# Splitting the dense matmuls of up and down into two 64-row matmuls, in a two-layer decoder kernel on one core

## The chip, the cores and the metric

The kernel runs on one core of a Trainium2 chip. The metric is device time in microseconds of one execution; lower is better.

## What is computed

Two layers act on 288 token columns (256 of a prompt, 32 of eight samples), d_model 1024. A layer adds to x the output of four token mixers (linear attention, spatial gating, a convolution module, sliding-window attention), gated and projected, and then a SwiGLU block. The change touches the second half alone:

```
x = x + merged @ w_out
g, up = split(rmsnorm(x, norm2_g) @ w_gate_up, 2)      # 1024 -> 2 x 2816
x = x + (silu(g) * up) @ w_down                        # 2816 -> 1024
```

## The kernel before, in words

Everything is kept transposed: features on the 128 partitions, the T = 288 tokens along the free axis. So a dense product is a row of tiles of 128 output features, and each tile accumulates over the input features in chunks of 128 (`u`): 8 chunks for `up` (KC), 22 for `down` (HC).

All arithmetic is float32 to the last bits that matter. An operand is split in two float32r parts, hi and lo, and each product of a chunk is three matmuls (lines 410 to 416, `split_mm`): w_hi by x_hi, w_hi by x_lo, w_lo by x_hi, all 128 x 128 weights by 128 x 288 columns into one PSUM bank. A tile of `up` is thus 24 matmuls, a tile of `down` 66. `up` has 44 tiles per layer, gate and up tiles alternating; `down` has 8.

The weights arrive in blocks through a ring of 4 slots. A block is one tile of `up`, or a third of a tile of `down` (6, 8 and 8 chunks). SyncE loads `raw` (512 KB) once w_lo of the block four earlier is done. ScalarE makes w_hi (`split`, line 785) once the block is there and the block four earlier is used up. In `up` and `down` VectorE makes w_lo = raw - w_hi (`split`, line 1132). TensorE waits for w_lo of each block (`wait_lo`), and for the bank of each tile (`bank_wait`). The tiles of `up` and `down` go round banks 0 to 3 (`t % 4`); banks 4 to 7 are free in these stages, except that the norm sums use bank 7 (`sum_of`, line 426: once behind tile 0 of `up` for the second norm, once early in the next layer).

The order on each engine is written out by hand, with semaphores between. In `up`, for each even (gate) tile t: VectorE multiplies the bank by the norm factor rs into `gate_s` (line 1549) and frees the bank; ScalarE takes its silu (line 1094) and then splits the weight blocks t+3 and t+4; VectorE makes w_lo of block t+3; POOL multiplies `gate_s` by rs again (line 1607). For each odd tile: VectorE multiplies the bank by `gate_s` into `hidden` (line 1554) and frees the bank, makes w_lo of block t+3; ScalarE copies `hidden` to h_hi (line 1098), VectorE forms h_lo (line 1557). In `down`, per tile: ScalarE splits three blocks, VectorE makes their three w_lo and adds the bank to x (line 1563). In layer 0 the squares and the norm of x for layer 1 follow tile by tile (lines 1002, 1013, 1147, and the additions of squares on POOL, line 1578). After the last tile of the kernel SyncE stores its part of x.

Matmuls with fewer rows exist in the mixers: the attention scores (lines 463 to 478) are plain float32 matmuls of 64 rows, alternating between partitions 0 to 63 and 64 to 127 and between two banks. Plain float32 products show in the profile as two matmuls each (a call of L449 five times is ten matmuls).

Of the kernel before, what the change touches and what calls it, by code (L numbers as in the profile page):

```python
# [29 lines left out]
T = SEQ + TS  # L30
KC = D_MODEL // P
HC = FFN // P
# [10 lines left out]
RING = 4  # L43
UNIT = P
# [6 lines left out]
U0 = O0 + KC  # L51
# [5 lines left out]
TU = TO + KC  # L57
TD = TU + 2 * HC
TILES = TD + KC
# [68 lines left out]
def trunk_program(nc, dram):  # L128
    f32, f32r = mybir.dt.float32, mybir.dt.float32r
    ACT, ALU, AX = mybir.ActivationFunctionType, mybir.AluOpType, mybir.AxisListType  # L130
    ctx = ExitStack()
    with ctx:
# [10 lines left out]
        h_hi = nc.alloc_sbuf_tensor_at("h_hi", [P, HC, T], f32r, offset=over_at)  # L143
        h_lo = nc.alloc_sbuf_tensor_at("h_lo", [P, HC, T], f32r, offset=over_at + 4 * HC * T)
# [9 lines left out]
        w_hi, w_lo = sb("w_hi", [RING, SLOT], f32r), sb("w_lo", [RING, SLOT], f32r)  # L154

        x = sb("x", [KC, T])
# [18 lines left out]
        rs = sb("rs", [T])  # L175
# [85 lines left out]
        def E(name):  # L261

            if name not in ev:
                ev[name] = sem(name)
            return ev[name]
# [22 lines left out]
        def wait_block(eng, l, b):  # L288

            eng.wait_ge(blocks_done, l * BLOCKS + b + 1)  # L290
# [5 lines left out]
        def wait_drained(eng, l, t):  # L296

            eng.wait_ge(bank_free[bank_of(t)], l * PER_BANK[bank_of(t)] + turn_of(t) + 1)

        def bank_wait(eng, l, t):  # L300

            before = l * PER_BANK[bank_of(t)] + turn_of(t)
            if before:
                eng.wait_ge(bank_free[bank_of(t)], before)
# [101 lines left out]
        def _(pe):  # L406
# [3 lines left out]
            def split_mm(out, slot, u, rh, rl, start, stop):  # L410

                wh = w_hi[:, slot, u * UNIT:(u + 1) * UNIT]
                wl = w_lo[:, slot, u * UNIT:(u + 1) * UNIT]
                pe.matmul(out, wh, rh, start=start, stop=False)  # L414
                pe.matmul(out, wh, rl, start=False, stop=False)  # L415
                return pe.matmul(out, wl, rh, start=False, stop=stop)  # L416

            def four_rows(bank, i, src):

                for j in range(4):  # L420
                    mm = pe.matmul(ps[TS * j:TS * j + TS, bank, i * P:(i + 1) * P], src, c("ident"), start=True, stop=True)
                return mm

            def sum_of(bank, src, event):

                pe.matmul(ps[:, bank, 0:T], c("ones"), src, start=True, stop=True).then_inc(E(event), 1)  # L426

            def mixers(l, l1):
# [3 lines left out]
                if l == 0:  # L432
                    pe.wait_ge(E("x_squared"), 1)
                else:
                    pe.wait_ge(squares, 2 * l * (KC - 1))
                sum_of(7, sq[:, 0, :], "n1_sums")
                yield from at("lr_sums")
                pe.wait_ge(E("w_lr_ready"), l1)
# [244 lines left out]
            for l in range(DEPTH):  # L683
                l1 = l + 1
# [53 lines left out]
                for t in range(2 * HC):  # L738
                    wait_lo(pe, g0 + U0 + t)
                    bank_wait(pe, l, TU + t)  # L740
                    for u in range(KC):
                        if t == 0:
                            pe.wait_ge(xl_done, x_part_at(l, N2 + u))
                        mm = split_mm(ps[:, t % 4, 0:T], (g0 + U0 + t) % RING, u, x_hi[:, u, :], x_lo[:, u, :], u == 0, u == KC - 1)
                    mm.then_inc(blocks_done, 1)
                    if t == 0:

                        pe.wait_ge(squares, (2 * l + 1) * (KC - 1))
                        sum_of(7, sq[:, 0, :], "n2_sums")

                for t in range(KC):
                    done = 0
                    for q, n in enumerate(DOWN_UNITS):
                        g = g0 + DN0 + 3 * t + q
                        wait_lo(pe, g)
                        if q == 0:
                            bank_wait(pe, l, TD + t)
                        for u in range(n):
                            if t == 0:
                                pe.wait_ge(hid_lo, l * HC + (done + u + 1))  # L760
                            mm = split_mm(ps[:, t % 4, 0:T], g % RING, u, h_hi[:, done + u, :], h_lo[:, done + u, :],
                                          done + u == 0, done + u == HC - 1)
                        done += n
                        mm.then_inc(blocks_done, 1)

# [2 lines left out]
        def _(act):  # L768
# [261 lines left out]
            for l in range(DEPTH):  # L1030
# [58 lines left out]
                act.wait_ge(stored, l1 * (16 * STORES_PER_LAYER))  # L1089
                for t in range(2 * HC):  # L1090
                    k = t // 2
                    wait_drained(act, l, TU + t)
                    if t % 2 == 0:
                        act.activation(gate_s[:, k % 2, :], gate_s[:, k % 2, :], ACT.Silu).then_inc(silu_done, 1)  # L1094
                        split(g0 + U0 + t + 3)
                        split(g0 + U0 + t + 4)
                    else:
                        act.activation(h_hi[:, k, :], hidden[:, k % 2, :], ACT.Copy).then_inc(hid_hi, 1)
                for t in range(KC):
                    for b in range(DN0 + 3 * t + 3, DN0 + 3 * t + 6):  # L1100
# [15 lines left out]
        def _(dve):  # L1116
# [4 lines left out]
            def link(ins, l):  # L1121

                ins.then_inc(dve_link, 1)
                chain[0] += 1
                dve.wait_ge(dve_link, chain[0])
# [33 lines left out]
            def bcast(ap, n):  # L1159

                return ap.unsqueeze(1).to_broadcast([P, n, ap.shape[1]])

            def conv(l, l1):

# [311 lines left out]
            for l in range(DEPTH):  # L1476
# [67 lines left out]
                dve.wait_ge(E("n2_rstd"), l1)  # L1544
                for t in range(2 * HC):
                    k = t // 2
                    wait_block(dve, l, U0 + t)
                    if t % 2 == 0:
                        dve.tensor_tensor(gate_s[:, k % 2, :], ps[:, t % 4, 0:T], rs[:, :], ALU.mult).then_inc(bank_free[t % 4], 1)  # L1549
                        split(g0 + U0 + t + 3)  # L1550
                    else:

                        dve.wait_ge(gate_ready, l * HC + (k + 1))
                        dve.tensor_tensor(hidden[:, k % 2, :], ps[:, t % 4, 0:T], gate_s[:, k % 2, :], ALU.mult).then_inc(bank_free[t % 4], 1)
                        split(g0 + U0 + t + 3)
                        dve.wait_ge(hid_hi, l * HC + (k + 1))
                        dve.tensor_tensor(h_lo[:, k, :], hidden[:, k % 2, :], h_hi[:, k, :].bitcast(f32), ALU.subtract)\
                            .then_inc(hid_lo, 1)
                for t in range(KC):
                    for b in range(DN0 + 3 * t + 3, DN0 + 3 * t + 6):  # L1560
                        split(g0 + b)
                    wait_block(dve, l, DN0 + 3 * t + 2)
                    dve.tensor_tensor(x[:, t, :], ps[:, t % 4, 0:T], x[:, t, :], ALU.add).then_inc(bank_free[t % 4], 1)
                    if t and l + 1 < DEPTH:
                        normed_part(x_part_at(l, NX + t - 1), 1, t - 1)
                if l + 1 < DEPTH:
# [195 lines left out]
```

## Time and profile before

| | |
|---|---|
| median of 3 runs | 1141.89 us (1140.75 to 1141.98) |
| profiled execution | 1141.02 us, its span 1139.2 us |
| TensorE (PE) busy, share of the span | 1112.4 us, 98% |
| weight loads (PEld) | 1079.6 us, 95% |
| VectorE (DVE) | 700.0 us, 61% |
| ScalarE (ACT) | 603.3 us, 53% |
| GpSimd (POOL) | 461.4 us, 41% |
| HBM traffic over the span | 160 GB/s |

The profile is of one execution. Busy time counts the union of an engine's records. Matmuls are pipelined, each record reaching into the next one's, so a busy TensorE may still have room; the distance between the starts of its matmuls tells more. `up` of layer 0 runs from about 365 to 506 us, its `down` to 576 us; `up` of layer 1 from about 925 to 1066 us, its `down` to 1136 us.

### The profile page before, as it was taken

What the parts mean: (1) busy time and instruction counts of PE and PEld (TensorE: products, weight loads), DVE (VectorE), ACT (ScalarE), POOL (GpSimd) and SP (SyncE); (2) the same over time, 40 slices, a digit from 0 to 9 for tenths busy, and PEclk for the clock granted to TensorE, in tenths of its full rate; (3) what the DMA queues carried; (4) which work ended last, traced back from release to release, by engine and by line L of the source; (5) the groups of instructions that cost most, each with busy time, mean ns of one, the idle gap of its engine ahead of it and who ended that gap; (6) DMA issues with size and microseconds to landing.
All of it is one profiled execution on the core that took longest, in us unless ns stands there. A gap on an engine that the chain in (4) does not pass through costs nothing.

```text
span 1139.2 us, 20187 instructions
## 1 busy us (share of the span) xinstructions
PE 1112.4 (98%) x8408; PEld 1079.6 (95%) x8408; DVE 700.0 (61%) x1017; ACT 603.3 (53%) x890; POOL 461.4 (41%) x250
## 2 busy tenths in 40 slices
PE   5999999999999999999999999999999999999999
PEld 5999899899999999999999998989999999999998
DVE  6678666743786555555548686675538755555543
ACT  5654565486545544444446564646766554444432
POOL 2676575466363111111167666545744531111000
PEclk9999999999999999999999999999999999999999
DMA  8654344244546576555544443433434555555652
GB/s 255 224 170 161 113 137 148 86 148 131 156 158 220 160 210 198 170 167 172 176 148 161 154 148 111 167 112 112 136 124 167 185 181 175 160 169 161 179 165 92
DMA packets 61483, 181.41 MB, mean 159 GB/s; under 512 B 16048, under 2 KB 18736, under 8 KB 60720
## 3 DMA queue, kind: packets, MB, share of 16 engines
q1 hardware_dynamic: 60816, 176.37, 48.5%
q10 hardware_dynamic: 576, 3.75, 0.9%
q8 instruction: 67, 1.10, 0.4%
q14 instruction: 24, 0.20, 0.1%
HBM read 174.85 MB, written 7.27 MB: 160 GB/s over the span
## 4 chain that ended last, share of the span: by engine, by line
PE 92%; ACT 3%; DVE 3%; issue 1%; DMA 1%; SPq 0%; ACTq 0%; DVEq 0%
PE ps L414 28%; PE ps L416 28%; PE ps L415 27%; DVE zg_r L1137 1%; ACT w_hi L785 1%; ACT work L863 1%; DMA raw<-in_w_z 1%; PE ps L516 0%; PE ps L426 0%; PE ps L500 0%; PE ps L449 0%; PE ps L454 0%; PE ps L677 0%; DVE work L1471 0%; DVE zg L1515 0%
## 5 line engine op out<-in xcount | busy, mean ns | idle before, releaser
L414 PE MATMUL ps<-x_hi,w_hi 128*128 128x288 f32 x1952 | 585.3, 300 | 14.8 <-DVE x_lo L1147 11.0
L415 PE MATMUL ps<-x_lo,w_hi 128*128 128x288 f32 x1952 | 576.9, 296 | 0.0
L416 PE MATMUL ps<-x_hi,w_lo 128*128 128x288 f32 x1952 | 575.2, 295 | 0.0
L785 ACT ACTIVATE w_hi<-raw 128x1024 fp32r<-128x1024 f32 x316 | 328.5, 1053 | 289.2 <-PE ps L416 274.7
L1583 POOL TENSOR_TENSOR w_lo<-raw,w_hi 128x1024 fp32r<-128x1024 f32 x131 | 339.2, 2602 | 213.2 <-ACT w_hi L785 213.0
L414 PEld LDWEIGHTS ps<-x_hi,w_hi 128*128 128x128 f32 x1952 | 367.0, 188 | 23.0 <-DVE w_lo L1132 10.9
L416 PEld LDWEIGHTS ps<-x_hi,w_lo 128*128 128x128 f32 x1952 | 368.7, 189 | 0.0
L415 PEld LDWEIGHTS ps<-x_lo,w_hi 128*128 128x128 f32 x1952 | 367.6, 188 | 0.8
L1132 DVE TENSOR_TENSOR w_lo<-raw,w_hi 128x1024 fp32r<-128x1024 f32 x185 | 229.5, 1241 | 138.6 <-ACT w_hi L785 138.3
L1607 POOL TENSOR_TENSOR work<-work,rs 128x288 f32<-128x288 f32 x44 | 35.9, 816 | 239.4 <-ACT work L1094 239.4
L416 PE MATMUL ps<-h_hi,w_lo 128*128 128x288 f32 x352 | 104.4, 296 | 0.0
L414 PE MATMUL ps<-h_hi,w_hi 128*128 128x288 f32 x352 | 104.0, 296 | 0.0
L415 PE MATMUL ps<-h_lo,w_hi 128*128 128x288 f32 x352 | 102.6, 292 | 0.0
L1209 DVE SCALAR_TENSOR_TENSOR ps<-hist_p,prm,ps 128x256 f32<-128x256 f32 x240 | 96.6, 483 | 0.2
L1094 ACT ACTIVATE work<-work 128x288 f32<-128x288 f32 x44 | 19.6, 444 | 111.5 <-DVE work L1549 111.5
L1602 POOL TENSOR_TENSOR zg<-zg 128x288 f32<-128x288 f32 x48 | 53.2, 1131 | 55.5 <-DVE zg L1515 55.3
L1578 POOL TENSOR_TENSOR work<-work 128x288 f32<-128x288 f32 x21 | 30.3, 1445 | 95.7 <-ACT work L1013 95.7
L415 PEld LDWEIGHTS ps<-h_lo,w_hi 128*128 128x128 f32 x352 | 67.1, 191 | 0.0
L414 PEld LDWEIGHTS ps<-h_hi,w_hi 128*128 128x128 f32 x352 | 66.1, 188 | 0.0
L416 PEld LDWEIGHTS ps<-h_hi,w_lo 128*128 128x128 f32 x352 | 66.0, 187 | 0.0
L414 PE MATMUL ps<-zg_r,w_hi 128*128 128x288 f32 x192 | 57.4, 299 | 2.9 <-DVE zg_r L1137 2.9
L416 PE MATMUL ps<-zg_r,w_lo 128*128 128x288 f32 x192 | 56.9, 296 | 0.0
(230 smaller groups left out, 1059.8 us busy)
## 6 DMA issues: line engine op xcount, KB each, us to landing
raw<-in_w_up SPq DMA_DIRECT2D x88, 512.0 KB, 4.1
raw<-in_w_z SPq DMA_DIRECT2D x68, 512.0 KB, 3.4
raw<-in_w_gate SPq DMA_DIRECT2D x64, 512.0 KB, 3.5
raw<-in_w_branch SPq DMA_DIRECT2D x32, 512.0 KB, 3.5
raw<-in_w_down SPq DMA_DIRECT2D x32, 512.0 KB, 3.7
raw<-in_w_out SPq DMA_DIRECT2D x16, 512.0 KB, 3.6
raw<-in_w_down SPq DMA_DIRECT2D x16, 384.0 KB, 3.2
kv<-in_state ACTq DMA_DIRECT2D x2, 1024.0 KB, 4.8
```

Source lines behind the costliest of these rows:

```text
L414: pe.matmul(out, wh, rh, start=start, stop=False)
L415: pe.matmul(out, wh, rl, start=False, stop=False)
L416: return pe.matmul(out, wl, rh, start=False, stop=stop)
L785: act.activation(w_hi[:, slot, :], raw[:, slot, :], ACT.Copy).then_inc(hi_done, 1)
L863: ins = act.activation(src[:, h, :], src[:, h, :], ACT.Exp, bias=small[:, 1, 8 * blk + h:8 * blk + h + 1], accum_out=small[:, 3, 8 * blk + ...
L1094: act.activation(gate_s[:, k % 2, :], gate_s[:, k % 2, :], ACT.Silu).then_inc(silu_done, 1)
L1132: dve.tensor_tensor(w_lo[:, slot, :], raw[:, slot, :], w_hi[:, slot, :].bitcast(f32), ALU.subtract)\
L1209: ins = dve.scalar_tensor_tensor(out=acc, in0=src, scalar=w, in1=acc, op0=ALU.mult, op1=ALU.add)
L1578: pool.tensor_tensor(sq[:, 0, :], sq[:, 0, :], sq[:, k, :], ALU.add).then_inc(squares, 1)
L1583: pool.tensor_tensor(w_lo[:, slot, :], raw[:, slot, :], w_hi[:, slot, :].bitcast(f32), ALU.subtract).then_inc(lo_pool, 1)
L1602: pool.tensor_tensor(gate[:, d, :], gate[:, d, :], gate[:, t, :], ALU.add).then_inc(summed, 1)
L1607: pool.tensor_tensor(gate_s[:, k % 2, :], gate_s[:, k % 2, :], rs[:, :], ALU.mult).then_inc(gate_ready, 1)
```

## The change

`halves_mm` takes the place of `split_mm` in `up` and `down`. Each of the three matmuls of a chunk becomes two: partitions 0 to 63 of weights and input into bank t % 4, partitions 64 to 127 into bank t % 4 + 4. Each of the two banks then holds half of the sum. Two waits are added on TensorE: the next layer's first norm sums (bank 7) wait for the last four tiles of `down` to be drained, and tile 3 of `up`, whose second bank is 7, waits for the second norm's factor.

The drain adds the two sums. An engine instruction of VectorE reads one bank and one SBUF tile here, so in `up` ScalarE first copies the lower bank to `gate_s` or `hidden`, and VectorE adds the upper bank to it (`halves_sum`), which frees both banks; the multiplications follow from SBUF, in place. In `down` VectorE makes two additions to x, the second waiting for the first.

```diff
+            def halves_mm(bank, slot, u, rh, rl, start, stop):
+
+                cols = slice(u * UNIT, (u + 1) * UNIT)
+                for w, v, first, last in ((w_hi, rh, start, False), (w_hi, rl, False, False), (w_lo, rh, False, stop)):
+                    for half in range(2):
+                        r = slice(64 * half, 64 * half + 64)
+                        mm = pe.matmul(ps[:, bank + 4 * half, 0:T], w[r, slot, cols], v[r], start=first, stop=last)
+                return mm
...
                     pe.wait_ge(squares, 2 * l * (KC - 1))
+                    for t in range(TILES - 4, TILES):
+                        wait_drained(pe, l - 1, t)
...
                     bank_wait(pe, l, TU + t)
+                    if t == 3:
+                        pe.wait_ge(E("n2_rstd"), l1)
...
-                        mm = split_mm(ps[:, t % 4, 0:T], (g0 + U0 + t) % RING, u, x_hi[:, u, :], x_lo[:, u, :], u == 0, u == KC - 1)
+                        mm = halves_mm(t % 4, (g0 + U0 + t) % RING, u, x_hi[:, u, :], x_lo[:, u, :], u == 0, u == KC - 1)
...
-                            mm = split_mm(ps[:, t % 4, 0:T], g % RING, u, h_hi[:, done + u, :], h_lo[:, done + u, :],
-                                          done + u == 0, done + u == HC - 1)
+                            mm = halves_mm(t % 4, g % RING, u, h_hi[:, done + u, :], h_lo[:, done + u, :],
+                                           done + u == 0, done + u == HC - 1)
...
(ScalarE, up)
-                    wait_drained(act, l, TU + t)
+                    wait_block(act, l, U0 + t)
+                    if t % 2 and k >= 2:
+                        act.wait_ge(hid_lo, l * HC + k - 1)
+                    act.activation((gate_s, hidden)[t % 2][:, k % 2, :], ps[:, t % 4, 0:T], ACT.Copy).then_inc(E("up_copied"), 1)
                     if t % 2 == 0:
+                        act.wait_ge(E("gate_scaled"), l * HC + k + 1)
                         act.activation(gate_s[:, k % 2, :], gate_s[:, k % 2, :], ACT.Silu).then_inc(silu_done, 1)
...
                     else:
+                        act.wait_ge(E("hidden_done"), l * HC + k + 1)
                         act.activation(h_hi[:, k, :], hidden[:, k % 2, :], ACT.Copy).then_inc(hid_hi, 1)
...
(VectorE)
+            def halves_sum(l, out, t):
+
+                dve.wait_ge(E("up_copied"), l * 2 * HC + t + 1)
+                dve.tensor_tensor(out, ps[:, 4 + t % 4, 0:T], out, ALU.add).then_inc(bank_free[t % 4], 1)
...
-                    wait_block(dve, l, U0 + t)
                     if t % 2 == 0:
-                        dve.tensor_tensor(gate_s[:, k % 2, :], ps[:, t % 4, 0:T], rs[:, :], ALU.mult).then_inc(bank_free[t % 4], 1)
+                        halves_sum(l, gate_s[:, k % 2, :], t)
+                        wait_drained(dve, l, TU + t)
+                        dve.tensor_tensor(gate_s[:, k % 2, :], gate_s[:, k % 2, :], rs[:, :], ALU.mult).then_inc(E("gate_scaled"), 1)
                         split(g0 + U0 + t + 3)
                     else:
+                        halves_sum(l, hidden[:, k % 2, :], t)
                         dve.wait_ge(gate_ready, l * HC + (k + 1))
-                        dve.tensor_tensor(hidden[:, k % 2, :], ps[:, t % 4, 0:T], gate_s[:, k % 2, :], ALU.mult).then_inc(bank_free[t % 4], 1)
+                        wait_drained(dve, l, TU + t)
+                        dve.tensor_tensor(hidden[:, k % 2, :], hidden[:, k % 2, :], gate_s[:, k % 2, :], ALU.mult)\
+                            .then_inc(E("hidden_done"), 1)
...
-                    dve.tensor_tensor(x[:, t, :], ps[:, t % 4, 0:T], x[:, t, :], ALU.add).then_inc(bank_free[t % 4], 1)
+                    link(dve.tensor_tensor(x[:, t, :], ps[:, t % 4, 0:T], x[:, t, :], ALU.add), l)
+                    dve.tensor_tensor(x[:, t, :], ps[:, 4 + t % 4, 0:T], x[:, t, :], ALU.add).then_inc(bank_free[t % 4], 1)
```

## Rows read from the trace of the kernel before

**Rows 1.** The page: TensorE's busy time; the chain that ended last, by engine and line.

```profile
PE 1112.4 (98%) x8408; PEld 1079.6 (95%) x8408; DVE 700.0 (61%) x1017; ACT 603.3 (53%) x890; POOL 461.4 (41%) x250
...
PE 92%; ACT 3%; DVE 3%; issue 1%; DMA 1%; SPq 0%; ACTq 0%; DVEq 0%
PE ps L414 28%; PE ps L416 28%; PE ps L415 27%; DVE zg_r L1137 1%; ACT w_hi L785 1%; ACT work L863 1%; DMA raw<-in_w_z 1%; PE ps L516 0%; PE ps L426 0%; PE ps L500 0%; PE ps L449 0%; PE ps L454 0%; PE ps L677 0%; DVE work L1471 0%; DVE zg L1515 0%
```

**Rows 2.** Timeline of TensorE inside `up`: start us, us, engine, line, operation.

```profile
450.00 0.30 PE L414 MATMUL ps<-x_hi,w_hi 128*128 128x288 f32 x1
...
451.60 0.30 PE L414 MATMUL ps<-x_hi,w_hi 128*128 128x288 f32 x1
...
450.00 0.19 PEld L415 LDWEIGHTS ps<-x_lo,w_hi 128*128 128x128 f32 x1
```

**Rows 3.** Windows in `up` and `down`: busy (count) PE, PEld, DVE, ACT, POOL; clock, DMA.

```profile
376.00:504.00 128.00, 128.00 (x963) 128.00 (x962) 73.11 (x101) 56.30 (x82) 16.36 (x20) 1.00 0.62 187
1073.00:1134.00 61.00, 61.00 (x463) 61.00 (x462) 26.48 (x26) 19.55 (x19) 0.00 (x0) 1.00 0.49 147
```

**Rows 4.** Timeline of TensorE in the first tile of the kernel.

```profile
12.07 0.44 PE L415 MATMUL ps<-x_lo,w_hi 128*128 128x288 f32 x1
12.31 0.44 PE L416 MATMUL ps<-x_hi,w_lo 128*128 128x288 f32 x1
```

**Rows 5.** Chain in order of time: start us, us until the next piece, what, matmuls.

```profile
75.00 2.44 PE ps L449 x10
...
94.51 1.09 PE ps L466 x16
95.60 0.87 PE ps L476 x8
96.47 0.33 PE ps L414
...
173.22 1.01 PE ps L421 x32
...
197.05 1.78 PE ps L585 x16
```

**Rows 6.** Groups by line, ScalarE's copy of a bank: busy us, mean ns | idle.

```profile
L790 ACT ACTIVATE zg<-ps,prm 128x288 f32<-128x288 f32 x52 | 25.2, 485 | 0.0
```

**Rows 7.** Timeline of VectorE and ScalarE in `up`.

```profile
448.60 0.46 DVE L1554 TENSOR_TENSOR work<-ps,work 128x288 f32<-128x288 f32 x1
448.97 1.22 DVE L1132 TENSOR_TENSOR w_lo<-raw,w_hi 128x1024 fp32r<-128x1024 f32 x1
450.10 0.45 DVE L1557 TENSOR_TENSOR h_lo<-work,h_hi 128x288 fp32r<-128x288 f32 x1
451.80 0.46 DVE L1549 TENSOR_TENSOR work<-ps,rs 128x288 f32<-128x288 f32 x1 [1.24 <-PE ps L416]
...
452.29 0.45 ACT L1094 ACTIVATE work<-work 128x288 f32<-128x288 f32 x1 [2.75 <-DVE work L1549]
452.64 1.99 ACT L785 ACTIVATE w_hi<-raw 128x1024 fp32r<-128x1024 f32 x2
```

**Rows 8.** Timeline at the start of `up`, layer 0: ScalarE, VectorE, TensorE's tile 3.

```profile
369.14 0.45 ACT L807 ACTIVATE rs<-rs 128x288 f32<-128x288 f32 x1
370.16 1.28 ACT L1094 ACT_TABLE_LOAD   x1 [0.57 <-DVE work L1549]
...
372.88 1.23 DVE L1132 TENSOR_TENSOR w_lo<-raw,w_hi 128x1024 fp32r<-128x1024 f32 x1 [2.80 <-ACT w_hi L785]
...
374.80 0.30 PE L414 MATMUL ps<-x_hi,w_hi 128*128 128x288 f32 x1
```

**Rows 9.** Timeline behind `down` of layer 0, and at the kernel's end.

```profile
577.45 0.81 POOL L1578 TENSOR_TENSOR work<-work 128x288 f32<-128x288 f32 x1 [1.57 <-ACT work L1013]
...
579.00 0.65 PE L426 MATMUL ps<-work,cst 128*128 128x288 f32 x2
...
1136.60 0.46 DVE L1563 TENSOR_TENSOR x<-ps,x 128x288 f32<-128x288 f32 x1 [8.27 <-PE ps L416]
```

## The prediction

> **What bounds the kernel now.** I read the page first. TensorE is busy 1112.4 of 1139.2 us, and 92% of the chain that ended last is TensorE, nearly all of it the three lines of `split_mm` [rows 1]. So the sum is one over TensorE's time, and over what makes it wait. Busy time cannot serve for this, because the records of neighbouring matmuls overlap (0.30 us each, 0.13 us apart). The number to read in the timeline is the distance between starts: from 450.00 to 451.60 us there are twelve matmuls in between, so 133.3 ns each, and the weight load of the next matmul starts together with the running one [rows 2]. A tile of `up` is 24 such matmuls, 3.20 us; a pair of tiles (gate, up) is 6.40 us. In `down` the window view has 463 matmuls in 61.00 us, 131.7 ns, the granted clock 1.00 in both stages [rows 3]. VectorE and ScalarE are busy 73.1 and 56.3 of 128 us in `up` [rows 3]: both have room in the mean, so the question for them is order, not sum.
>
> What is 133.3 ns made of? In the very first tile the same instructions start 240 ns apart [rows 4], which is what 288 columns take at the lower level of 1.2 GHz; at 2.4 GHz that would be 120. So 13 ns of every dense matmul are something other than streaming columns. Whether half-row matmuls keep, lose or double this is the question of the case.
>
> **The change, part by part.**
>
> (1) The matmuls. 2 layers x 44 tiles x 24 = 2112 in `up` and 2 x 8 x 66 = 1056 in `down`, 3168 in all, become 3168 pairs. If the halves of a pair ran one after the other, each at the price of a whole one, this alone would add 3168 x 133 ns = 421 us. The trace has the same arrangement already. L476 issues 64-row matmuls on alternating row groups into different banks: 8 in 0.87 us, so 4 pairs at 217 ns for 256 columns of plain f32. A full 128-row matmul in plain f32 (L449) takes 2.44/10 = 244 ns for 288 columns, 217 for 256. A pair costs what one whole matmul costs [rows 5]. No row shows a 64-row matmul on the split operands (one pass at full rate); from both sides, its pair costs between 120 ns (half of rows 4) and 266 ns (two whole ones). I take 133.3, the dense value, since in plain f32 pair and whole agree and each half streams as many columns as the whole. Change: 0.
>
> Here a rule speaks against expecting a gain. The Trainium skill says in "TensorE: Matmul & The Clock Gate", in the table of "Why this matters for your kernels", that one K=32 matmul takes the same time as K=128 and that the gain is tile concurrency: cutting a full-height matmul buys nothing. By it the sum stays at 0 for this term.
>
> (2) Issue. TensorE gets four instructions (two loads, two matmuls) per 133 ns, 33 ns each, against 67 before. In L421 32 matmuls and their loads pass in 1.01 us, 16 ns each; L466 and L476 together are 48 instructions in 1.96 us, 41 ns each, bound by their own streaming [rows 5]. I count 0; these bursts are short, so a sustained rate is not shown, and that stays among the risks.
>
> (3) Changes of array form. Eight pairs of L466 should take 8 x 111 = 0.89 us (L585, whole matmuls of the same 128 columns: 1.78/16 = 111 ns) and take 1.09: entering the 64-row form costs 0.20. The L414 after it takes 0.33 instead of 0.13: leaving costs 0.20 [rows 5]. Each layer has the entry into `up`, out and in again for the n2 sums after tile 0, and layer 0 also the way out behind `down`: 7 changes, 1.4 us on TensorE's path. Between 0 and 0.33 each, 0 to 2.3 us.
>
> (4) The drain in `up`. Per tile ScalarE gets a copy from PSUM (0.485 us, as L790 [rows 6]) and VectorE an addition; the multiplications then read SBUF. As the orders are written this ties both engines into one loop per pair of tiles: VectorE sum, multiply; ScalarE silu, two weight splits, copy of the odd tile; VectorE sum, multiply, w_lo, h_lo, then the next sum. From start to start an addition takes 448.97-448.60 = 0.37 us and w_lo 450.10-448.97 = 1.13; one that waits for the other's end takes 0.46 plus 0.04 (L1549 at 451.80, silu at 452.29, so 0.49); silu takes 0.35 to the next instruction, and two splits end 1.99 after the first begins, with an overlap of 0.1, so about 0.945 each [rows 7]. The loop: 0.50 + 0.49 + 0.35 + 0.945 + 0.945 + 0.52 (copy and hop) + 0.50 + 0.37 + 1.13 + 0.37 = 6.12 us, against TensorE's 6.40. The cover is 0.28 us per pair, so it costs nothing as long as TensorE stays at 133 ns, and it is what a faster TensorE would hit. Banks come free about 1 us after a tile's end and are wanted again three tiles later (9.6 us).
>
> (5) Start of `up`. The silu of tile 0 comes later by the copy and the sum (ScalarE free at 369.49, copy to 369.97, sum to 370.46, multiply to 370.95), with the table load behind it: silu at 372.3 and not, as now, at the load's end at 371.45. w_lo of block 3 then starts at 373.7 instead of 372.88 and ends at 374.95; TensorE wants it at 374.80 [rows 8]. But the three form changes ahead put that at 375.4, and two of them delay the n2 sums too, so w_lo is there at 375.35. I take 0.2 us per layer, 0.4; ends 0 and 1.7 (0.85 twice).
>
> (6) `down`. The drain has two linked additions, 0.50 us more. Inside the stage the next tile's 8.7 us hide it. At the end of layer 0 the last x part is late by 0.5: POOL's last addition of squares, now 577.45 to 578.26, slides to 578.8, and TensorE wants it at 579.00 [rows 9]; hidden, and if that cover went it would cost at most 0.5. At the very end nothing hides it: the last addition starts at 1136.60 and takes 0.46 [rows 9], the second one comes behind it with its hand-over, so +0.5. The added waits of TensorE (n2_rstd ahead of tile 3; the last four tiles drained ahead of the next n1 sums) are met by then: the one 5 us early (369.6 against 374.80 [rows 8]), the other whenever the squares are, which need the same additions. Nothing queues behind them. No DMA is added or moved; the loads wait for w_lo and follow it.
>
> **Sum.** 0 + 0 + 1.4 + 0 + 0.4 + 0.5 = +2.3 us. The profiled execution took 1141.02 us (1.8 outside the span) and would become 1143.3; the median shown is 1141.89, 0.9 above it, so I forecast 1144.2 us. A measurement of this kernel tells about 0.2%, 2.3 us, from no change: the forecast sits on that edge.
>
> **The rivals.**
>
> A, the halves run faster than the whole (0.28). The 13 ns over the 120 belong to changing weights under a full-rate stream; if the load for one row group can go on while only the other streams, they shrink. Against it: L466 and L585 show no such gain in plain f32, and the load already starts with the running matmul [rows 2, 5]. For it: plain f32 has no 13 ns excess to lose (244 is twice 122), so those rows cannot show it. In `up` the gain stops at the 6.12 us loop: 44 x 0.28 = 12.3 us; in `down` (131.7 - 121) x 1056 = 11.3, with 121 between half of 240 and half of 244. With +2.3: 1141.9 - 23.6 + 2.3 = about 1121 us. It decides as soon as a pair takes less than 133.3 - 2.3/3.168 = 132.6 ns. The Trainium skill's page "TensorE: Matmul & The Clock Gate", section "Part 3: Packing small matmuls — row/col tiling", says a weight load overlaps a running matmul only when the row group differs. That is a rule for this rival, but the trace does not agree with its strict form: whole-height loads begin with the running matmul [rows 2]; if they waited for its 120 ns of columns, 133 could not be reached.
>
> B, the pair costs more than the whole (0.12): the two starts are some ns apart and the full-rate stream does not absorb it. At 140 ns a pair, 3168 x 7 = 22 us: 1166 us.
>
> C, the loop of (4) is longer than 6.40 (0.06): its ten steps each 0.05 us longer than I count give 6.6; 44 x 0.2 = 9 us: 1153 us.
>
> D, the change does not do what it says (0.06): the halves go one after the other, because this operand type or TensorE's issue does not allow the overlap. 1142 + 3168 x 107 to 133 = 1480 to 1565 us.
>
> **How the numbers follow.** The forecast's mechanism has 0.48; its sum can be 0.5 to 5 us (terms 3, 5 and 6 at their ends), so 0.25 of it lies within 0.2% and 0.23 above. A gives 0.27 faster and 0.01 same; B 0.12, C 0.05 and D 0.06 slower, C 0.01 same. Faster 0.27, same 0.27, slower 0.46. The likeliest case alone spans 1142 to 1147. The range for 8 in 10 reaches down to A in full, 1120, and up to B, 1166; left out are D, the upper half of B and the little beyond A.
>
> **What would show it.** Right: starts of the A halves 133 ns apart in `up` with the B half within some ns, pairs of tiles at 6.40 us, VectorE idle some 0.3 us per pair ahead of the sum, extra gaps of 0.2 us at the form changes. A: pair distance of 120 to 130 ns in `down`, and in `up` waits of TensorE for w_lo with pairs at 6.12. B: 135 to 145 ns with no waits. C: waits for w_lo while the pair distance stays 133. D: B halves starting 107 ns or more after A halves. The forecast falls if the distance in `down`, where no other engine is near its limit, is not 131 to 134 ns.

## The result, and the profile after

Six runs of the changed kernel have a median of 1147.36 us (1145.70 to 1149.67), six of the kernel before 1141.93 us. The ratio is 1.0049, with a 95% interval of 1.0031 to 1.0066: slower by about 5.4 us. The forecast was 1144.2 in a range of 1120 to 1166, with slower as the likeliest sign. The size needs a second look, because only a third of it is work that the change adds.

First the page of the profiled execution (1148.73 us, span 1146.9). It answers to [rows 1]:

```profile
PE 1118.2 (97%) x11576; PEld 1083.2 (94%) x11576; DVE 747.7 (65%) x1121; ACT 633.8 (55%) x978; POOL 461.1 (40%) x250
...
PE 91%; DVE 4%; ACT 4%; issue 1%; DMA 1%; SPq 0%; ACTq 0%; DVEq 0%
```

TensorE has 3168 more matmuls (11576 against 8408) and is busy 5.8 us longer. The timeline in `up` shows where they went, against [rows 2]:

```profile
451.78 0.30 PE L424 MATMUL ps<-x_lo,w_hi 64*128 64x288 f32 x2
451.91 0.30 PE L424 MATMUL ps<-x_hi,w_lo 64*128 64x288 f32 x2
452.05 0.30 PE L424 MATMUL ps<-x_hi,w_hi 64*128 64x288 f32 x2
452.18 0.30 PE L424 MATMUL ps<-x_lo,w_hi 64*128 64x288 f32 x2
```

Two matmuls (x2) fill one row of 0.30 us, so the two of a pair start almost together (one alone shows 0.29), and the rows stand 0.13 us apart, as whole matmuls did. The windows, to be laid beside [rows 3], have 1924 and 928 matmuls where there were 963 and 463:

```profile
376.00:504.00 128.00, 128.00 (x1924) 128.00 (x1922) 91.68 (x143) 69.86 (x120) 16.31 (x20) 1.00 0.57 185
1080.00:1141.00 61.00, 61.00 (x928) 61.00 (x926) 29.67 (x33) 19.92 (x19) 0.00 (x0) 1.00 0.51 154
```

Next, where the 7.7 us between the two spans are. The table takes each stage from the start of the last matmul of the stage before it to the start of its own last matmul, in the two timelines.

| stage | before, us | after, us | difference |
|---|---|---|---|
| layer 0, up to the end of `out` | 364.60 | 364.45 | -0.15 |
| layer 0, up | 141.26 | 141.87 | +0.61 |
| layer 0, down | 69.81 | 69.81 | 0.00 |
| layer 1, z | 131.86 | 132.05 | +0.19 |
| layer 1, gate | 135.31 | 141.26 | +5.95 |
| layer 1, branch and out | 82.36 | 82.36 | 0.00 |
| layer 1, up | 141.26 | 141.86 | +0.60 |
| layer 1, down | 69.81 | 69.81 | 0.00 |
| from the last matmul to the end | 2.9 | 3.4 | +0.5 |

The stages with half-row matmuls give 0.6 + 0.6, the way out of `down` 0.2, the last drain 0.5. The largest entry lies in the gate stage of layer 1, which the change does not touch. Windows there (same columns as above) show what happened:

```profile
732.00:737.00 5.00, 5.00 (x52) 3.91 (x50) 0.46 (x1) 3.07 (x6) 1.21 (x1) 0.66 0.77 289
753.00:760.50 7.50, 7.50 (x54) 6.97 (x54) 4.74 (x15) 0.52 (x2) 0.65 (x1) 0.54 0.25 83
737.00:753.00 16.00, 14.69 (x130) 14.03 (x126) 13.64 (x16) 9.53 (x15) 9.46 (x4) 1.00 0.34 116
```

The granted clock, the third number from the right, fell twice to its lower level of 1.2 GHz. Ahead of both falls TensorE was in the short matmuls of the mixers; ahead of the second it had also idled 1.31 us for VectorE. Whole matmuls then start 240 ns apart, as in [rows 4]; the prediction had read those as the lower level from their distance alone:

```profile
755.81 0.44 PE L415 MATMUL ps<-x_lo,w_hi 128*128 128x288 f32 x1
756.05 0.44 PE L416 MATMUL ps<-x_hi,w_lo 128*128 128x288 f32 x1
756.29 0.44 PE L414 MATMUL ps<-x_hi,w_hi 128*128 128x288 f32 x1
```

The 0.6 us per layer in `up` are at the changes of array form. Each matmul row that follows such a change stands further from the next:

```profile
364.45 0.29 PE L416 MATMUL ps<-zg_r,w_lo 128*128 128x288 f32 x1
364.68 0.40 PE L424 MATMUL ps<-x_hi,w_hi 64*128 64x288 f32 x2
364.91 0.30 PE L424 MATMUL ps<-x_lo,w_hi 64*128 64x288 f32 x2
365.05 0.30 PE L424 MATMUL ps<-x_hi,w_lo 64*128 64x288 f32 x2
```

From 364.45 to 364.68 and on to 364.91 are 0.23 us each in place of 0.13: 0.2 us for one change. It comes three times at the start of `up`, and once behind `down` of layer 0 (+0.19 in the table).

The drain keeps up. VectorE's rows of one pair of tiles, beside [rows 7]:

```profile
452.02 0.45 DVE L1584 TENSOR_TENSOR h_lo<-work,h_hi 128x288 fp32r<-128x288 f32 x1
452.69 0.46 DVE L1184 TENSOR_TENSOR work<-ps,work 128x288 f32<-128x288 f32 x1 [0.23 <-ACT work L1108]
453.19 0.46 DVE L1573 TENSOR_TENSOR work<-work,rs 128x288 f32<-128x288 f32 x1
455.10 1.23 DVE L1150 TENSOR_TENSOR w_lo<-raw,w_hi 128x1024 fp32r<-128x1024 f32 x1 [1.46 <-ACT w_hi L798]
...
459.09 0.46 DVE L1184 TENSOR_TENSOR work<-ps,work 128x288 f32<-128x288 f32 x1 [0.22 <-ACT work L1108]
```

The sum of the gate tile starts every 6.40 us, TensorE's period, and VectorE idles 0.23 us ahead of it. That is nearly the whole reserve: the 1.46 us of idle time ahead of w_lo are a wait for ScalarE inside the loop of the prediction's part (4). How much the loop leaves is measured further down.

At the end the two additions and the store, beside [rows 9]:

```profile
1143.82 0.46 DVE L1590 TENSOR_TENSOR x<-ps,x 128x288 f32<-128x288 f32 x1 [7.78 <-PE ps L424]
1144.31 0.46 DVE L1591 TENSOR_TENSOR x<-ps,x 128x288 f32<-128x288 f32 x1
1144.79 0.33 SPq L401 DMA_DIRECT2D out_y<-x  x1
```

### The profile page after: what moved, and what is told of

Read it like the earlier page. It is cut to its first block, busy times and chain, and to the rows that moved or that the text cites. A ratio compares the mean times of both kernels' runs of the same rounds, so it can differ in the third digit from the quotient of the medians.

```text
span 1146.9 us, 26757 instructions
## 1 busy us (share of the span) xinstructions
PE 1118.2 (97%) x11576; PEld 1083.2 (94%) x11576; DVE 747.7 (65%) x1121; ACT 633.8 (55%) x978; POOL 461.1 (40%) x250
## 4 chain that ended last, share of the span: by engine, by line
PE 91%; DVE 4%; ACT 4%; issue 1%; DMA 1%; SPq 0%; ACTq 0%; DVEq 0%
PE ps L424 37%; PE ps L414 16%; PE ps L416 15%; PE ps L415 15%; DVE zg_r L1155 1%; ACT w_hi L798 1%; ACT work L876 1%; DMA raw<-in_w_z 1%; PE ps L435 1%; PE ps L527 0%; PE ps L511 0%; PE ps L460 0%; PE ps L465 0%; PE ps L688 0%; DVE work L1494 0%
## 5 line engine op out<-in xcount | busy, mean ns | idle before, releaser
L414 PE MATMUL ps<-x_hi,w_hi 128*128 128x288 f32 x1248 | 377.6, 303 | 14.7 <-DVE x_lo L1165 10.8
L415 PE MATMUL ps<-x_lo,w_hi 128*128 128x288 f32 x1248 | 370.1, 297 | 0.0
L416 PE MATMUL ps<-x_hi,w_lo 128*128 128x288 f32 x1248 | 369.0, 296 | 0.0
L416 PEld LDWEIGHTS ps<-x_hi,w_lo 128*128 128x128 f32 x1248 | 236.8, 190 | 0.0
L424 PE MATMUL ps<-x_hi,w_hi 64*128 64x288 f32 x1408 | 211.2, 293 | 0.0
L424 PE MATMUL ps<-x_lo,w_hi 64*128 64x288 f32 x1408 | 210.1, 292 | 0.0
L424 PE MATMUL ps<-x_hi,w_lo 64*128 64x288 f32 x1408 | 209.4, 291 | 0.0
L424 PEld LDWEIGHTS ps<-x_hi,w_lo 64*128 64x128 f32 x1408 | 135.1, 185 | 0.0
L424 PEld LDWEIGHTS ps<-x_hi,w_hi 64*128 64x128 f32 x1408 | 133.9, 184 | 1.1 <-issue 1.1
L424 PEld LDWEIGHTS ps<-x_lo,w_hi 64*128 64x128 f32 x1408 | 134.1, 184 | 0.0
```

Of the source, the lines that this page charges most:

```text
L424: mm = pe.matmul(ps[:, bank + 4 * half, 0:T], w[r, slot, cols], v[r], start=first, stop=last)
```

## The experiments

The theory is the forecast's: a half-row pair costs what a whole matmul costs, and the change pays for the changes of array form and the last drain. Open was the clock: whether the change brings the falls, by starting layer 1 later (S) or by its 64-row matmuls (U), or whether they come to the kernel before as well (T).

### The changed kernel again

> The changed kernel once more, unchanged. Of the profiled difference of +7.7 us in the span, 1.4 us sit at the changes of array form, 0.5 us at the last drain, and 5.8 us in the gate stage of layer 1, where the granted clock fell twice to its lower level; no other stage differs. Theory S (the fall comes with the later start of layer 1): runs at +1.9 us when the clock stays at 1.00, and at +4 to +8 us when it falls; the mixers of layer 1 show it again, those of layer 0 do not. Rival T (a chance event with no tie to the change): the kernel before shows such falls as often as this one.

Twelve runs: median 1145.96 us, 1142.55 to 1150.14. The profiled one (1148.58 us) has the two falls of the clock in the gate stage of layer 1 again, at the same places, and none in layer 0. The kernel before ran 35 times beside the first four experiments: median 1142.15, 1140.61 to 1147.01. The ratio is 1.0021 (1.0002 to 1.0041), less than half of the first difference. Each run lists its mean granted clock, and the times follow it:

| kernel | runs at clock 1.000 | their times, median | all runs: n, mean clock |
|---|---|---|---|
| before | 13 | 1140.61 to 1141.30, 1140.85 | 35, 0.9984 |
| changed | 3 | 1142.55 to 1142.72, 1142.64 | 12, 0.9973 |
| shifted (below) | 1 | 1141.59 | 12, 0.9982 |
| halves in up alone | 2 | 1142.36, 1142.60 | 12, 0.9972 |
| tile 0 whole | 6 | 1141.73 to 1142.30, 1141.89 | 12, 0.9986 |

At full clock the changed kernel is 1.8 us slower (1142.64 - 1140.85), as the stages say with their +1.9. But the kernel before falls too, in 22 of its 35 runs (the changed one in 9 of 12), with eight at a clock of 0.995 or 0.996 and 1146.55 to 1147.01 us. That is near T's expectation. Where the clock fell in those runs is not known: the one trace kept of the kernel before has no fall.

### The kernel before, with layer 1 shifted

```diff
+                if l + 1 < DEPTH:
+                    for _ in range(4):
+                        pe.matmul(ps[:, 6, 0:64], c("ones"), c("ident")[:, 0:64], start=True, stop=True)
```

> The kernel before, with whole matmuls everywhere, and eight short plain matmuls (64 columns) behind down of layer 0, so that layer 1 starts 0.8 to 1.0 us later. They compute nothing that is used. Theory S: the clock falls in the mixers of layer 1 as in the changed kernel, so +3 to +8 us with a mean clock below 0.999 in most runs. Rival T, and rival U (the 64-row matmuls themselves bring it on): +0.8 to +1.0 us, clock 1.000.

The shift is 0.9 us (z of layer 1 takes 132.76 in place of 131.86), the one run at clock 1.000 took 1141.59, +0.7 against the kernel before. Median 1144.77, ratio 1.0018 (1.0004 to 1.0032). The profiled execution had its fall in the first tiles of layer 0, ahead of the shift, and none in layer 1, so this trace does not bear S out. It does not refute it either: the slowest run (1147.51 us, clock 0.995) has no trace, and S had asked for a clock below 0.999 in most runs, where 5 of 12 have one. Of the 12 runs 11 show some fall, against 22 of 35 before; that is too few to say that a shift draws falls.

### Halves in up alone

```diff
-                            mm = halves_mm(t % 4, g % RING, u, h_hi[:, done + u, :], h_lo[:, done + u, :],
-                                           done + u == 0, done + u == HC - 1)
+                            mm = split_mm(ps[:, t % 4, 0:T], g % RING, u, h_hi[:, done + u, :], h_lo[:, done + u, :],
+                                          done + u == 0, done + u == HC - 1)
...
-                    link(dve.tensor_tensor(x[:, t, :], ps[:, t % 4, 0:T], x[:, t, :], ALU.add), l)
-                    dve.tensor_tensor(x[:, t, :], ps[:, 4 + t % 4, 0:T], x[:, t, :], ALU.add).then_inc(bank_free[t % 4], 1)
+                    dve.tensor_tensor(x[:, t, :], ps[:, t % 4, 0:T], x[:, t, :], ALU.add).then_inc(bank_free[t % 4], 1)
```

> Halves in up alone; down has its whole matmuls and its single addition again. By the forecast's terms: eight changes of array form (into up, out, in, and out before down, per layer) at 0.20 us, 1.6 us, and no longer end: +1.6 us at clock 1.00, with down at 69.8 us as in both kernels. Layer 1 starts 0.8 us late as well, so theory S expects the clock to fall here too; rival U expects it if the halves of up are enough. If a half-row pair of down were dearer than a whole matmul, down would be shorter here than in the changed kernel; I expect no difference above 0.1 us.

The runs at clock 1.000 took 1142.36 and 1142.60, +1.6 over the kernel before, as the terms say. `up` takes 141.87 and 141.86, `down` 70.01 us in both layers, 0.2 more than in either kernel: the way out of the 64-row form now lies in it. That is more than the 0.1 us of difference that was expected, but it is the price of one change of form, which the expectation had counted without placing it in `down`. The matmuls of `down` are thus no cheaper whole than in halves. Median 1145.77, ratio 1.0030 (1.0011 to 1.0049), with falls of the clock in 10 of 12 runs. Whether the halves of `up` draw them (U) is not decided by this.

### Tile 0 of up whole

```diff
+                        if t == 0:
+                            mm = split_mm(ps[:, 4 * (u % 2), 0:T], (g0 + U0) % RING, u, x_hi[:, u, :], x_lo[:, u, :], u < 2, u >= KC - 2)
+                            continue
                         mm = halves_mm(t % 4, (g0 + U0 + t) % RING, u, x_hi[:, u, :], x_lo[:, u, :], u == 0, u == KC - 1)
```

> As the changed kernel, but tile 0 of up keeps whole matmuls (even chunks in one bank, odd chunks in the other, so that the drain stays the same). The second norm's sums then come before the first half-row matmul: one change of array form at the start of up in place of three. Term 3 of the forecast (0.20 us per change): up is 0.40 us shorter per layer than in the changed kernel, 141.46 against 141.87 us, and the span 0.8 us shorter at equal clock. Rival: the 0.6 us per layer come from the later w_lo of block 3 (term 5): then up stays at 141.9 us. Layer 1 starts 0.4 us later than in the kernel before; theory S gives no number for that shift.

`up` takes 141.47 us in both layers, 0.40 less than in the changed kernel, and the median at clock 1.000 is 1141.89, 0.75 less. One change of form in place of three per layer: 0.2 us each, shown. The ratio is 1.0008 (0.9992 to 1.0025): this version cannot be told from the kernel before, and its full-clock runs are still 1.0 us slower.

### One half left out

```diff
                     for half in range(2):
+                        if half and w is w_hi and not first:
+                            continue
+                        if half and w is w_lo and not last:
+                            continue
                         r = slice(64 * half, 64 * half + 64)
```

> As the changed kernel, but of the matmuls on rows 64 to 127 of up and down only the first and the last of each tile are left (that they write the bank at all); the other products of these rows are left out of the sums. The forecast's theory, that the second half runs wholly beside the first: starts of the first halves stay 133 ns apart, up stays at 141.9 us and down at 69.8 us per layer. Rival: the second halves cost part of the 133 ns (a half-height matmul alone would be cheaper, 120 to 127 ns): up 128 to 135 us, down 63 to 67 us.

`down` takes 69.81 us, just as with both halves, and `up` 141.85 (141.86 in layer 1), against 141.87 and 141.86. The matmuls of the first half stand as far apart alone as with their partners:

```profile
449.90 0.29 PE L428 MATMUL ps<-x_hi,w_hi 64*128 64x288 f32 x1
450.04 0.29 PE L428 MATMUL ps<-x_lo,w_hi 64*128 64x288 f32 x1
450.17 0.29 PE L428 MATMUL ps<-x_hi,w_lo 64*128 64x288 f32 x1
450.31 0.29 PE L428 MATMUL ps<-x_hi,w_hi 64*128 64x288 f32 x1
```

So 133 ns are the price of one stream of 288 columns with its weight load, with 64 rows as with 128. The second half is free. The run took 1147.03 us at a clock of 0.997, with falls in the first tiles and in the mixers of layer 0, which end 4.3 us later than in the changed kernel. A detail for later: the last matmul on rows 64 to 127 of `up` starts 0.4 us ahead of the last one on rows 0 to 63, although the program has it behind.

### Three and three

```diff
-                for w, v, first, last in ((w_hi, rh, start, False), (w_hi, rl, False, False), (w_lo, rh, False, stop)):
-                    for half in range(2):
-                        r = slice(64 * half, 64 * half + 64)
+                for half in range(2):
+                    r = slice(64 * half, 64 * half + 64)
+                    for w, v, first, last in ((w_hi, rh, start, False), (w_hi, rl, False, False), (w_lo, rh, False, stop)):
```

> The same matmuls as in the changed kernel in another order: the three of rows 0 to 63 of a chunk, then the three of rows 64 to 127. Theory: matmuls start in program order, and two on the same row group are 133 ns apart, so of six only the third with the fourth and the sixth with the next first run side by side: 4 steps of 133 ns per chunk in place of 3, 1056 chunks x 133 ns = +141 us over the changed kernel. Rival 1: TensorE takes them out of order and nothing changes. Rival 2: side by side needs strict alternation of the weight loads too, then all six are in a row: +421 us.

Nothing changes: `up` 141.87, `down` 69.81, the run took 1143.83 us at a clock of 0.999. The theory of this experiment, start in program order, is wrong. The rows are still pairs, each of two matmuls that read the same tiles (the trace does not name the rows), although the program puts all three of the lower rows first:

```profile
450.01 0.30 PE L424 MATMUL ps<-x_lo,w_hi 64*128 64x288 f32 x2
450.14 0.30 PE L424 MATMUL ps<-x_hi,w_lo 64*128 64x288 f32 x2
450.28 0.30 PE L424 MATMUL ps<-x_hi,w_hi 64*128 64x288 f32 x2
```

### Half a tile and half a tile

```diff
-                    for u in range(KC):
+                    for half in range(2):
+                        for u in range(KC):
...
-                        mm = halves_mm(t % 4, (g0 + U0 + t) % RING, u, x_hi[:, u, :], x_lo[:, u, :], u == 0, u == KC - 1)
+                            mm = halves_mm(t % 4, (g0 + U0 + t) % RING, u, x_hi[:, u, :], x_lo[:, u, :], u == 0, u == KC - 1, (half,))
```

> As the changed kernel, but in up all 24 matmuls of rows 0 to 63 of a tile are issued before the 24 of rows 64 to 127; down stays alternating. The run with three and three showed that TensorE starts the two row groups side by side although the program has them one after the other. How far does this go? Theory W, a window: TensorE looks ahead over a limited number of instructions (in the trace of the kernel before its waits pass about 34 instructions ahead of the matmuls); 24 matmuls and 24 weight loads are more than that, so part of each half tile runs alone, and up gets longer by 10 to 70% (156 to 240 us per layer). Rival 1, no limit that matters: up stays at 141.9 us. Rival 2, no overlap at this distance at all: up doubles, 282 us.

`up` takes 245.66 us in both layers, 104 more, and the run 1350.41 us. It is theory W, with less reach than I gave it: the time lies outside the expected 156 to 240. Where one half tile ends, rows of two appear, and then single ones again:

```profile
402.01 0.29 PE L424 MATMUL ps<-x_hi,w_lo 64*128 64x288 f32 x1
402.02 0.42 PE L424 MATMUL ps<-x_hi,w_hi 64*128 64x288 f32 x2
402.25 0.32 PE L424 MATMUL ps<-x_lo,w_hi 64*128 64x288 f32 x2
402.39 0.31 PE L424 MATMUL ps<-x_hi,w_lo 64*128 64x288 f32 x2
402.52 0.29 PE L424 MATMUL ps<-x_hi,w_hi 64*128 64x288 f32 x1
...
404.79 0.42 PE L424 MATMUL ps<-x_hi,w_hi 64*128 64x288 f32 x2
```

A half tile takes 404.79 - 402.02 = 2.77 us, where 24 matmuls alone would take 3.20: about three of them run beside the other half's. At the end of `up`, where the names of the inputs tell the two stages apart, the order itself can be seen. The first matmul of `down` (h_hi, rows 0 to 63) starts ahead of the last three of `up` (rows 64 to 127), which stand before it in the program:

```profile
609.77 0.40 PE L424 MATMUL ps<-h_hi,w_hi 64*128 64x288 f32 x1
...
610.16 0.29 PE L424 MATMUL ps<-x_hi,w_lo 64*128 64x288 f32 x1
```

That is why three and three cost nothing, and it shows what a half-row matmul costs that finds no partner: nearly all of its 133 ns.

### 256 columns

```diff
+                if narrow:
+                    out, rh, rl = out[:, 0:256], rh[:, 0:256], rl[:, 0:256]
```

> The kernel before with whole matmuls, but in down and in the tiles 4 to 43 of up each takes 256 of the 288 columns (the 32 sample columns are left out there). What the 13 ns over the 120 ns of streaming are. Theory F, a fixed price per change of weights: 256 columns take 106.7 + 13.3 = 120 ns. Theory R, a slower stream: 256 x 133.3/288 = 118.5 ns. Theory L, the weight load is the bound: 133 ns stay. In down, 1056 matmuls: F -13.9 us, R -15.2 us over both layers, L 0.

`down` takes 62.77 us, 7.05 less for 528 matmuls: 13.35 ns each, the 32 columns at 2.4 GHz (13.33) and nothing else. That is F: a fixed 12.2 ns on top of the columns, at 288 (132.2) and at 256 (118.9). `up` takes 126.35, 14.91 less for 960 matmuls: 15.5 ns each, 117.8 ns a matmul, a little under R's 118.5. L is refuted. F and R are both out as a single rule: some 11 to 13 ns stay on top of the columns, and they move by one or two ns with the stage, for a reason that no run here shows.

```profile
449.72 0.28 PE L416 MATMUL ps<-x_hi,w_hi 128*128 128x256 f32 x1
...
450.90 0.28 PE L417 MATMUL ps<-x_lo,w_hi 128*128 128x256 f32 x1
```

Ten matmuls in 1.18 us. The run took 1102.69 us and had a fall of the clock in the gate stage of layer 1, +5.95 us there, the same two falls as in the changed kernel, with whole matmuls in all of `up` and `down`. The largest entry of the first table thus comes without the change's half-row matmuls, and what is left open is only how often.

### The drain without the halves

```diff
-                for w, v, first, last in ((w_hi, rh, start, False), (w_hi, rl, False, False), (w_lo, rh, False, stop)):
-                    for half in range(2):
-                        r = slice(64 * half, 64 * half + 64)
-                        mm = pe.matmul(ps[:, bank + 4 * half, 0:T], w[r, slot, cols], v[r], start=first, stop=last)
+                half = n_chunk % 2
+                for w, v, first, last in ((w_hi, rh, n_chunk < 2, False), (w_hi, rl, False, False), (w_lo, rh, False, n_chunk >= count - 2)):
+                    mm = pe.matmul(ps[:, bank + 4 * half, 0:T], w[:, slot, cols], v, start=first, stop=last)
```

> The drain of the changed kernel without its half-row matmuls: whole matmuls, those of even chunks into the lower bank and those of odd chunks into the upper one, added as in the changed kernel. By the forecast's terms 3, 4 and 6: no change of array form, the drain hidden, and the last drain 0.5 us longer: up 141.3 us and down 69.8 us per layer as in the kernel before, span +0.5 us at clock 1.00. Rival: part of the 0.6 us per layer in up comes from the longer drain, then up is above 141.3 us.

`up` takes 141.26 us in both layers and `down` 69.81, exactly as in the kernel before. The copies and additions cost nothing, and all of the 0.6 us is the array form. The run took 1142.71 us with a clock fall (0.998) in the first tiles of layer 0, so its total does not show the +0.5 by itself; from its last matmul to the end it takes 3.4 us, as the changed kernel does, against 2.9 before.

### How near the loop is

```diff
-                        mm = pe.matmul(ps[:, bank + 4 * half, 0:T], w[r, slot, cols], v[r], start=first, stop=last)
+                        mm = pe.matmul(ps[:, bank + 4 * half, 0:n], w[r, slot, cols], v[r, 0:n], start=first, stop=last)
```

Here n is 256 in the tiles 4 to 43 of `up`.

> The changed kernel with 256 of the 288 columns in the matmuls of the tiles 4 to 43 of up (the sample columns are left out there); the drain keeps its 288 columns. With whole matmuls and the old drain this took 117.8 ns a matmul in up, a pair of tiles 5.65 us, up 126.4 us. It tests term 4: the loop over VectorE and ScalarE was worked out as 6.12 us per pair, and with the copy at its measured 0.39 us as 6.03. If that loop is the bound, up takes about 13.4 + 20 x 6.03 less 2 to 3 us of start slack, 131 to 134 us, with waits of TensorE for w_lo or of the banks. Rival: the loop is not closed as I read it, and up is 127.0 us (126.4 and 0.6 of form changes).

`up` takes 134.28 us, 7.9 more than the same columns with whole matmuls and the old drain (126.35); 0.6 of that are the form changes. It is also 0.3 above the expected 131 to 134, and `down` starts with a backlog and takes 70.66. The run took 1129.42 us at full clock, the kernel before beside it 1140.76. The loop holds TensorE back, with these rows on VectorE:

```profile
443.59 0.45 DVE L1184 TENSOR_TENSOR work<-ps,work 128x288 f32<-128x288 f32 x1
444.08 0.46 DVE L1573 TENSOR_TENSOR work<-work,rs 128x288 f32<-128x288 f32 x1
...
447.24 0.46 DVE L1184 TENSOR_TENSOR work<-ps,work 128x288 f32<-128x288 f32 x1
447.81 0.46 DVE L1580 TENSOR_TENSOR work<-work 128x288 f32<-128x288 f32 x1
...
449.69 0.45 DVE L1184 TENSOR_TENSOR work<-ps,work 128x288 f32<-128x288 f32 x1
```

and these waits of TensorE (us in total, times, longest) between 376 and 480 us:

```profile
PEld ps L424 <- DVE w_lo L1150: 4.6, 14, 0.4
PE ps L424 <- DVE w_lo L1150: 0.2, 1, 0.2
```

The sum has no idle time ahead of it any more, and the period is 449.69 - 443.59 = 6.10 us, against 6.12 forecast before anything was run (the 6.03 put in its place was worse). The mean over all pairs of `up` is 6.09.

## Why the prediction was right, and where it was not

**Term 1, the pair at 133.3 ns: right.** `down` is the same to 0.01 us with halves and whole, and `up` is the same apart from the form changes. The reading of plain f32 pairs in [rows 5] carried over to the split operands, which no row had shown. The rule of the Trainium skill that a small-K matmul takes as long as a full one ("TensorE: Matmul & The Clock Gate", the table of "Why this matters for your kernels", which says it of K=32) is borne out here for 64 rows: the matmuls of one half alone stand 133 ns apart. In `down` the distance is 69.81/528 = 132.2 ns; the 131.7 of the prediction came from a window whose 463 matmuls include some that only reach into it, and rival A was priced 0.5 us too low by that.

**Term 2, issue: right.** 1924 matmuls in 128 us with as many weight loads is an instruction every 33 ns, sustained.

**Term 3, seven form changes at 0.2 us: right,** 0.61 + 0.19 + 0.60 = 1.4 us, and taking two away per layer gave 0.40 back.

**Term 4, the loop of 6.12 us: right.** It measured 6.10, so the reserve is 0.30 us per pair, where 0.28 was forecast. Two of its steps were off and cancel: from the start of the odd tile's copy (446.82) to its sum (447.24) are 0.42 us and not 0.52, and its multiplication starts 0.57 us behind the sum (447.81) and not 0.50. Correcting the one without the other is what made 6.03 worse; that 6.12 came so close is in part luck.

**Term 5, the late start of up, 0.4 us: wrong, it is 0.** The copy is shorter than I took it (0.39, not 0.485), and above all the table load does not stand behind the sum. These rows answer to [rows 8]:

```profile
369.74 0.39 ACT L1108 ACTIVATE work<-ps 128x288 f32<-128x288 f32 x1
370.15 1.28 ACT L1111 ACT_TABLE_LOAD   x1
371.44 0.45 ACT L1111 ACTIVATE work<-work 128x288 f32<-128x288 f32 x1
```

The load runs while VectorE adds and multiplies, so the silu starts at 371.44, as before, and not at 372.3, and w_lo of block 3 at 372.87, where it started at 372.88. The step of the prediction that failed is this order, load behind multiplication.

**Term 6, the last drain +0.5 and the layer boundary hidden: right.** The additions start 0.49 us apart.

**The sum** was 2.3 us and measured 1.8 between runs at full clock. The rest of the 5.4 us is what the forecast had no term for: it took a clock of 1.00 for granted on both sides. The profile before showed 1.00 throughout, and three runs within 1.2 us gave no hint; 35 runs show the kernel before between 1140.6 and 1147.0. In the six runs of the first comparison the changed kernel was at 0.994 to 0.999 and the kernel before mostly near its full-clock time. The measured 1147.36 lies inside the wide range, but just above the 1142 to 1147 that the prediction gave its own mechanism, and the sign "slower" came out as clearly as it did because of the falls; 1.8 us are 0.16%. That part is luck.

Whether the change makes falls more frequent or longer stays open. Counted by runs without a fall, three of 12 against 13 of 35 says nothing. Counted by what the falls cost in the mean, over each kernel's full-clock time, the changed kernel pays more both times: 5.0 us (1147.59 - 1142.64) against 1.2 (1142.04 - 1140.85) in the first six runs, 3.3 (1145.99 - 1142.64) against 2.3 (1143.10 - 1140.85) in the second comparison. That is a hint, and no run here shows a mechanism for it: the runs of the two kernels overlap, and the fall in the gate stage also comes with whole matmuls in `up` and `down`.

**The rivals.** A fell: in no stage did the pairs come closer than the whole matmuls. The excess over streaming is real (11 to 12 ns of it at 256 columns), but a half alone has the same 133 ns as a pair, so both halves of a pair pay it at the same time. The strict rule behind A, which the Trainium skill has in "TensorE: Matmul & The Clock Gate", "Part 3: Packing small matmuls — row/col tiling", would have given a gain; the measurement (69.81 us in `down` either way) decides against it. B, C and D fell with the distance of 133 ns and the loop at 6.10.

## What to carry to other kernels

Splitting full-height matmuls over row groups bought nothing here: the halves run side by side, but one full matmul does the work of both in the same 133 ns, and the change of array form (0.2 us each) and the second drain come on top. Before giving work to engines off the critical path, add up the loop that their waits on each other close, and compare it with the bound's period; the sum of busy shares (72% for VectorE in `up`) did not show that less than 5% were left (6.10 us of 6.40). And compare runs of equal granted clock: two medians can differ by more than the change does.

## What was not expected of the hardware

TensorE starts matmuls of different row groups out of program order. With the three of one half written ahead of the three of the other, they still ran in pairs; with 24 and 24 about three ran ahead, and `down` started at 609.77 while `up` had its last start at 610.16. The Trainium skill says in "TensorE: Matmul & The Clock Gate", section "Part 3: Packing small matmuls — row/col tiling", that matmuls start and end strictly in program order; here it does not hold across row groups; within one, no trace shows the contrary.

The granted clock of this single-core kernel falls in some executions and not in others, in both kernels: by up to 6.2 us over the full-clock time before (1147.01 against 1140.85) and 7.5 changed (1150.14 against 1142.64). In the traces it fell in the first tiles (at 21 us, behind about 2 us in which TensorE waited for VectorE) or in the short matmuls of the mixers (at 733 and 753 us, and at 172 us in one run). Ahead of the fall at 733 us TensorE was never idle (busy 5.00 of the 5.00 us from 728 to 733).
